# One kernel, other places: where activations, weight ring and weight halves begin in a partition

## The reference

```python
for l in range(DEPTH):                                   # first block
    proj = h @ w_in[l]                                   # then mla, multiscale_pool, mlstm
    mix = jnp.concatenate([a, p, m], axis=-1) @ w_out[l]
    h = layer_norm(ALPHA * h + mix, ln1_g[l], ln1_b[l])
    a, g = jnp.split(h @ w_up[l], 2, axis=-1)            # 1024 -> 2 x 2816
    f = (silu(causal_dwconv(g, w_fconv[l], b_fconv[l])) * a) @ w_down[l]
    h = layer_norm(ALPHA * h + f, ln2_g[l], ln2_b[l])
for l in range(DEPTH):                                   # second block
    proj = modulate(rmsnorm(x, norm_mix_g[l]), sh1, sc1) @ w_in[l]   # then conv and attention
    x = x + g1 * (jnp.concatenate([y_conv, y_att], axis=-1) @ w_out[l])
    h = modulate(rmsnorm(x, norm_ffn_g[l]), sh2, sc2)
    f = swiglu(h, ...) if l == 0 else moe_swiglu(h, ...) # dense 2816; 8 experts of 3584, 2 per row
    x = x + g2 * f
```

## Time and profile before

| | us |
|---|---|
| median of 3 runs | 2156.11 |
| lowest, highest | 2154.88, 2157.43 |
| span of the profiled execution | 2153.0 |
| PE busy in it | 2105.8 |
| DVE busy | 1784.9 |
| ACT busy | 1371.5 |

### The profile page before, as it was taken

The page is one execution under the profiler, slowest core; times in us unless marked ns, Lnnn a source line. Parts: engine busy times, 40 slices in busy tenths (PEclk is TensorE's granted clock), DMA queues, the critical chain, the costliest instruction groups (busy, mean ns, idle before and its releaser), DMA issues.

```text
span 2153.0 us, 31152 instructions
## 1 busy us (share of the span) xinstructions
PE 2105.8 (98%) x12690; PEld 1857.1 (86%) x12690; DVE 1784.9 (83%) x2305; ACT 1371.5 (64%) x1930; POOL 2.1 (0%) x16
## 2 busy tenths in 40 slices
PE   8999999999999999999999999999999999999998
PEld 7899999899998889999888888888888888888886
DVE  5778886788888977766978898898988889888987
ACT  4555544555545664445657777777777777777775
POOL 0000000000000000000000000000000000000000
PEclk9999999999999999999998999999999999999999
DMA  5358784347785417765318999989998999999994
GB/s 192 120 192 278 240 282 177 121 189 269 242 285 200 156 59 274 259 218 209 138 59 307 367 360 352 348 348 360 355 350 346 355 366 352 350 344 361 369 354 179
DMA packets 89429, 574.88 MB, mean 267 GB/s; under 512 B 10049, under 2 KB 10049, under 8 KB 31041
## 3 DMA queue, kind: packets, MB, share of 16 engines
q1 hardware_dynamic: 87984, 566.89, 70.9%
q0 software_dynamic: 288, 3.15, 0.4%
q10 hardware_dynamic: 1008, 2.79, 0.3%
HBM read 571.75 MB, written 1.05 MB: 266 GB/s over the span
## 4 chain that ended last, share of the span: by engine, by line
PE 83%; DVE 11%; ACT 3%; DMA 1%; issue 1%; DVEq 0%; ACTq 0%
PE bank L2042 45%; PE bank L485 37%; DVE wlo L1399 2%; DVE arena L1790 2%; PE bank L2100 1%; DVE RSTD L1465 1%; ACT whi L1012 1%; DMA ring<-in_w_in 0%; DMA side<-in_w_ada 0%; DVE XC L1474 0%; DVE arena L1535 0%; ACT arena L1297 0%; ACT HH L1067 0%; DVE arena L1532 0%; DVE XC L1454 0%
## 5 line engine op out<-in xcount | busy, mean ns | idle before, releaser
L1399 DVE TENSOR_TENSOR wlo<-ring,whi 128x1024 fp32r<-128x1024 f32 (+1 forms) x766 | 875.8, 1176 | 126.8 <-ACT whi L1012 120.3
L1012 ACT ACTIVATE whi<-ring 128x1024 fp32r<-128x1024 f32 (+1 forms) x766 | 760.1, 1021 | 211.6 <-PE bank L485 127.3
L485 PE MATMUL bank<-HH,whi 128*128 128x256 f32 x1536 | 439.9, 286 | 5.3 <-DVE wlo L1399 3.8
L485 PE MATMUL bank<-HH,wlo 128*128 128x256 f32 x1536 | 433.3, 282 | 0.0
L485 PE MATMUL bank<-HL,whi 128*128 128x256 f32 x1536 | 432.4, 281 | 0.0
L485 PEld LDWEIGHTS bank<-HH,whi 128*128 128x128 f32 x1536 | 291.6, 190 | 10.7 <-DVE wlo L1399 4.7
L485 PEld LDWEIGHTS bank<-HL,whi 128*128 128x128 f32 x1536 | 291.6, 190 | 0.9 <-issue 0.5
L485 PEld LDWEIGHTS bank<-HH,wlo 128*128 128x128 f32 x1536 | 291.6, 190 | 0.0
L1399 DVE TENSOR_TENSOR extra_lo<-ring,extra_hi 128x1024 fp32r<-128x1024 f32 x224 | 264.2, 1220 | 14.8 <-ACT extra_hi L1012 14.5
L1012 ACT ACTIVATE extra_hi<-ring 128x1024 fp32r<-128x1024 f32 x224 | 229.8, 1060 | 42.9 <-PE bank L2042 42.9
L2042 PE MATMUL bank<-whi,xg 128*128 128x512 f32 x672 | 221.1, 397 | 0.0
(11 more groups left out here) (292 smaller groups left out, 3564.8 us busy)
## 6 DMA issues: line engine op xcount, KB each, us to landing
ring<-in_moe_gate SPq DMA_DIRECT2D x112, 1024.0 KB, 5.4
ring<-in_moe_up SPq DMA_DIRECT2D x112, 1024.0 KB, 6.5
ring<-in_moe_down SPq DMA_DIRECT2D x112, 1024.0 KB, 5.1
side<-in_w_ada SPq DMA_DIRECT2D x96, 512.0 KB, 4.1
ring<-in_w_up SPq DMA_DIRECT2D x44, 1024.0 KB, 4.8
ring<-in_w_in SPq DMA_DIRECT2D x32, 1024.0 KB, 5.4
ring<-in_w_down SPq DMA_DIRECT2D x32, 704.0 KB, 5.3
ring<-in_ffn_gu SPq DMA_DIRECT2D x22, 1024.0 KB, 4.8
```

Source lines behind the costliest of these rows:

```text
L485: return pe.matmul(out, lhsT, rhs, start=start, stop=stop, skip_group_check=True)
L1012: a.activation(hi, part, ACT.Copy).then_inc(*made.up(("hi", n, i)))
L1399: v.tensor_tensor(lo, part, hi.bitcast(F32), ALU.subtract).then_inc(*done.up(("lo", n, i)))
```

## The change

Tiles are allocated in another order and with small gaps between them. `at_line` takes up as many bytes as are missing to a wanted remainder modulo 256. The small tiles and `vec` come first, then `ring` and the activations at remainder 32, then HH, `side` and the arena at 32, last `whi` and `wlo` at 96; `HALF` grows to 1088 numbers, 4352 bytes, a multiple of 256, so that all four places have one remainder. The two extra places are moved to remainder 96 within what they are laid over. The list of instructions of each engine, their order, sizes and waits are the same as before; only addresses differ.

| tile | before, mod 256 | after, mod 256 |
|---|---|---|
| ring, xT, hT (and xg_ht), XC, SQ, RS, RSTD, cst | 128 | 32 |
| HH (and xg_hh), HL | 224 | 32 |
| side, ring_2 | 224 | 32 |
| arena: midh, midl, xg0, xg1, hsh, hsl, ysh, selt | 32 | 32 |
| whi, wlo, places 0 and 2 | 224 | 96 |
| whi, wlo, places 1 and 3 | 96 | 96 |
| extra_hi, extra_lo, place 4 | 128 | 96 |
| extra_hi, extra_lo, place 5 | 160 | 96 |

```diff
--- before.py
+++ after.py
@@ -26,7 +26,9 @@
 NSLOT = 4
 NHALF = 4
 NHALF_MOE = 6
-HALF = 1056
+HALF = 1088
+ACT_LINE = 32
+WEIGHT_LINE = 96
 BIG = 1.0e30
 TAPS = 8
 
@@ -127,6 +129,20 @@
         def sem(name):
             return ctx.enter_context(nc.semaphore(name))
 
+        def at_line(residue, name):
+
+            gap = (residue - -(-nc.sbuf_base // 32) * 32) % 256
+            if gap:
+                sb(name, [128, gap], mybir.dt.uint8)
+
+        vec = sb("vec", [128, VEC_N])
+        modT = sb("modT", [128, DEPTH, 48])
+        amod = sb("amod", [128, 2, 8])
+        cact = sb("cact", [128, 8])
+        small = sb("small", [128, 128])
+        icnt = sb("icnt", [128, 1], I32)
+        idx8 = sb("idx8", [128, 2, 8], U32)
+        at_line(ACT_LINE, "pad_ring")
         ring_t = sb("ring", [128, NSLOT, SLOT])
         xT = sb("xT", [128, 8, S])
         hT_at = -(-nc.sbuf_base // 32) * 32
@@ -139,28 +155,25 @@
         assert nc.sbuf_base == hT_at + 4 * (3 * 2048 + 6 * S)
         cst_at = -(-nc.sbuf_base // 32) * 32
         cst = sb("cst", [128, CST_N])
-        vec = sb("vec", [128, VEC_N])
+        at_line(ACT_LINE, "pad_hh")
         HH_at = -(-nc.sbuf_base // 32) * 32
         HH = sb("HH", [128, 8, S], F32R)
         HL = sb("HL", [128, 8, S], F32R)
         assert nc.sbuf_base == HH_at + 4 * 2 * 2048
-        whi = sb("whi", [128, NHALF, HALF], F32R)
-        wlo = sb("wlo", [128, NHALF, HALF], F32R)
         side_at = -(-nc.sbuf_base // 32) * 32
         side = sb("side", [128, 3072])
         assert nc.sbuf_base == side_at + 4 * 3072
         side_2 = sb("side_2", [128, 1024])
         assert nc.sbuf_base == side_at + 4 * 4096
-        modT = sb("modT", [128, DEPTH, 48])
-        amod = sb("amod", [128, 2, 8])
-        cact = sb("cact", [128, 8])
-        small = sb("small", [128, 128])
-        icnt = sb("icnt", [128, 1], I32)
-        idx8 = sb("idx8", [128, 2, 8], U32)
         AREN = 14336
         base = -(-nc.sbuf_base // 32) * 32
         arena = sb("arena", [128, AREN])
         assert nc.sbuf_base == base + 4 * AREN
+        at_line(WEIGHT_LINE, "pad_whi")
+        whi = sb("whi", [128, NHALF, HALF], F32R)
+        wlo = sb("wlo", [128, NHALF, HALF], F32R)
+        for at_ in (hT_at, HH_at, base):
+            assert at_ % 256 == ACT_LINE
 
         def over(name, at, *shape):
             return nc.alloc_sbuf_tensor_at(name, [128, *shape], F32R, offset=base + 4 * at)
@@ -175,8 +188,11 @@
         PSEL = nc.alloc_sbuf_tensor_at("psel", [128, 2, NE, 128], F32R, offset=hT_at + 4 * 2048)
         YSL = nc.alloc_sbuf_tensor_at("ysl", [128, 1024], F32R, offset=hT_at + 4 * 4096)
 
-        extra_at = [hT_at + 4 * (2 * 2048 + 1024), cst_at + 4 * (-(-CST_HEAD // 8) * 8)]
-        assert 4 * (-(-CST_HEAD // 8) * 8 + 2048) <= 4 * CST_N
+        def weight_line(at_):
+            return at_ + (WEIGHT_LINE - at_) % 256
+
+        extra_at = [weight_line(hT_at + 4 * (2 * 2048 + 1024)), weight_line(cst_at + 4 * CST_HEAD)]
+        assert extra_at[0] + 4 * 2048 <= cst_at and extra_at[1] + 4 * 2048 <= cst_at + 4 * CST_N
         EXTRA = [[nc.alloc_sbuf_tensor_at(f"extra_{x}{i}", [128, 1024], F32R, offset=at_ + 4096 * (x == "lo"))
                   for i, at_ in enumerate(extra_at)] for x in ("hi", "lo")]
         HSH = [over(f"hsh{i}", 12288 + 512 * i, 4, 128) for i in range(2)]
```

## The result

| | before | after |
|---|---|---|
| median of 4 runs, us | 2155.49 | 2144.0 |
| lowest, highest | 2154.56, 2157.43 | 2142.72, 2144.45 |
| span of the profiled execution | 2153.0 | 2140.8 |

The ratio is 0.9939, with a 95% interval from 0.9927 to 0.9951. The kernel is faster by 11.5 us; I forecast 33.6 us less. The sign holds, the size doesn't: about one third of the gain came, and the time is near rival A's 2147.5.

The account below looks back on a forecast made before the run. PE was taken as the bound: for about nine tenths, matmul count times start-to-start step. Savings of 17.5 + 6.1 + 0.5 + 9.5 = 33.6 us gave 2153.0 - 33.6 + 3.1 = 2122.5 us, range 2110 to 2150.

Parts of the forecast that it names:

- rival A: Slow step stays: HH products gain 5.3 us, midh lose 6.2, experts gain 9.5; 2147.5 us, chance 0.17.
- What bounds the kernel: Whole kernel: PE's matmul count times start-to-start step is about nine tenths of the time; other engines and DMA still fit.
- Rival B: Wide stretches: engines feeding PE become the bound, half the HH gain turns into waits for wlo; 2134.5 us, chance 0.06.
- The three comparisons: PE trace of before: HH halves 118.3 beside 120.0 ns, midh 113.3, experts 230.0 to 235.0, read as effects of places.
- Rival C: All PE products: no effect, the step follows the kind of product and not the place; 2156 us, chance 0.11.
- Part 1: Products moving HH or HL: 119.2 to 113.4 ns each, saving 17.5 us in wide stretches and 6.1 in projections.
- My own complication: Midh stretches: one pair of places allows two steps; breaks bring the slow one, escapes come at weight changes 224 to 96.
- Part 2: Products moving midh or midl: most already at 113.3 ns, only slow halves after breaks gain, 0.5 us.
- Part 3: Experts' 4032 matmuls of 512 columns: 232.5 to 230.0 ns each, 10.1 us saved, taken as 9.5.
- Part 4: Everything else: DVE's splits stay at 1220 ns, ACT's taken alike, f32 products left out; 0 us.
- The sum: Whole kernel: 17.5 + 6.1 + 0.5 + 9.5 = 33.6 us saved, giving 2122.5 us.

Follow-up runs that it names:

- alt_halves: Kernel after with HALF back at 1056, so weight halves lie at 96 and 224 in turn, extra places at 96: 2130.88 us, ratio to before 0.9882.
- split_swapped: Kernel after with experts' weights at 32 and other weight halves at 96 and 224 in turn, 96 first: 2119.66 us, ratio to before 0.9825.
- split_by_stage: Kernel after with experts' weights at 32 and other weight halves at 224 and 96 in turn, 224 first: 2122.33 us, ratio to before 0.9835.

## Why the prediction was wrong

**What bounds the kernel, and that the clock, DVE, ACT and DMA leave room.** Right. PE has no gap in any stretch shown, and where HH did run at 113.3 (alt_halves) DVE carried 91% without a loss there. Rival B didn't come about; even in the fastest version steps and spans differ by only 2 to 3 us.

**The three comparisons.** What the rows said was right: places set the step. The fixed runs show it without any other difference between the kernels: 2144.0 to 2175.28 us for the same instructions. Rival C does not hold: moving nothing but the weight halves from difference 64 to 160 costs 31 us. I had taken two pages of the Trainium skill for it: "SBUF — State Buffer", section "Who interferes with whom", says that PE never waits on anyone, and "TensorE: Matmul & The Clock Gate", section "Step-by-step: what each phase is for", says that loading the next weights takes no read bandwidth from the running matmul. My conclusion from them, that places cost nothing, is refuted. The statements themselves are not: no run shows which of PE's reads slow each other, if any do, and in the stretches compared PE waits for no other engine.

**Part 1, the step that failed.** I saved 119.2 - 113.4 = 5.8 ns on each product of HH. Measured: 119.1 to 117.0, 2.1 ns; the starts of all HH products sum to 556.9 us before and 548.1 after, 8.8 us gained where 23.6 were forecast. The 5.8 took the fast step for the step of the pair 32 against 96. My own complication said that the pair has two, that a break brings the slow one, and that every escape is at a change of weights from 224 to 96. I then read the escapes as leading to a good pair, where they hang on the change itself. The change made all places alike and with that took away the only thing that released the slow step within a row; the fast rows that are left, 5 of the 22 of over 90 products, were fast soon after their start. The rows that I took for proof, the fast halves of midh in the earlier trace rows, were fast because of the alternation that the change removes. Experiment 1 shows it from the other side: give the alternation back, and each row of over 90 HH products reaches the forecast's step, at the latest after two halves.

**Part 2.** I counted 0.5 us gained; it is a loss of 4.7 us (180.7 to 185.4 us over the starts; 114.1 to 117.3 ns). This is the same mistake: midh already had the alternation of 64 and 192 and lost it.

**Part 3.** Right: 232.4 to 229.8 ns, 4032 x 2.6 = 10.5 us, forecast 10.1 and entered as 9.5. The experts' products show no such pair of steps that I could find; their halves differ by place alone, as I had read them. But 64 was not their best: 0 gives 227.4, 9.7 us more. The trace of before had 0 only with xg_hh, whose third product in each group of three is at 96 with xg_ht; the 139 steps from 0 to 0 there average 231.2 ns, so that trace didn't show what 0 throughout would give.

**Part 4.** Right for the splits: they keep 1220 ns. The other products are in the sum below.

**The sum.** 8.8 - 4.7 + 10.5 = 14.6 us; the span fell by 12.2. By their starts, waits included, the products of 512 columns gave 9.9 us and not 10.5; the products of all other kinds, which part 4 had at nothing, took 1.3 us more, and what lies behind the last matmul 0.5: 8.8 - 4.7 + 9.9 - 1.3 - 0.5 = 12.2. Rival A had this mechanism and its parts (5.3 gained on HH, 6.2 lost on midh, 9.5 on the experts) and came within 3.5 us; the HH products that ran fast after a restart, which it didn't have, are 0.18 x 4571 x 4.5 ns = 3.7 us. I gave it 0.17 because 10 of 13 changes released at once. That was a count of changes, not of rows without a change, and of those the trace of before held no long one. That trace also held more of the slow step than the prediction tells: midh doesn't begin with it at 298.62, but has it in all products from 288.86 to 300.73, the halves at 96 from 291.16 and 296.84 included, as at 613.96.

**Open.** What in the chip makes two steps possible at 64 and 192, and why only the change from 224 to 96 releases, and not always the first, no run here shows. Which restarts bring the fast step isn't settled either: the same break, two f32 products with xT, is followed by a fast row at 118.01 and at 439.07 us of the kernel after, and in split_swapped by a slow one at 119.62 and a fast one at 434.94.

## What to carry to other kernels

When the pace of an engine is read from a stretch, ask how that stretch got there: a pace that appears only after a change of operands may belong to the change and not to the operands. Before unifying what alternates, look whether the alternation does work. And in a kernel that is an unbroken row of matmuls, the first bytes of its operands are worth a scan of a few builds for each kind of product apart: here two kinds wanted opposite places, and the same instructions took from 2119.7 to 2175.3 us.

## What the runs showed of the hardware that I had not expected

- The step of a float32r matmul depends on where its operands begin modulo 256. With activations at 32 and the weights 0 to 192 further on, the slow steps are 117.3 to 120.0 ns with 256 columns of activations moving; with 512 columns of weights moving the means are 227.4 (difference 0) to 234.1 ns (difference 160), at a granted clock of 1.00.
- The order of the differences isn't the same for the two: 0 is, with 160, the slowest for 256 columns with the weights standing and the fastest for 512 with the weights moving.
- At 64 and 192, and only there, a second step of 113.3 ns exists beside 117.8. A row holds one of them for up to 527 products. Going from 192 to 64 released the slow one in 27 of 36 cases among the midh products, going from 64 to 192 in none of 20. When two halves lay ahead, the first such change always did it in rows of over 90 products; when one did, sometimes only the second. Of all such changes 10 of 13 released in before, 8 of 14 in split_by_stage. Going between 64 and 0 never did.
